# A two-layer encoder trunk with expert layers: plain fp32 products for gathering expert rows and scattering expert outputs

## The chip, the cores and the metric

The kernel runs on one core of a Trainium2 chip. The metric is the device time of one execution in microseconds; for the kernel before, three timed runs are at hand, and one more execution that the hardware profiler took. All rows and stretches shown are of that profiled execution, and their clock starts at its first instruction.

## The reference

A trunk of two layers works on 256 tokens of width 1024, all in float32. Layer 0 mixes by retention and chunked attention, layer 1 by sliding-window attention. Each layer has then a mixture of 16 experts, and after it a gated addition of a side input. What the change touches is the mixture:

```python
g_onehot = jax.nn.one_hot(argmax(g_logits), 4)          # one of 4 groups
top_v, top_i = lax.top_k(e_sel, 2)                      # two of its 4 experts
gates = g_onehot[:, :, None] * (g_w[:, None] * e_gate)[:, None, :]
for gi in range(4):
    hg = jnp.einsum('td,edf->tef', t, w_gate[gi])       # 1024 -> 512
    hu = jnp.einsum('td,edf->tef', t, w_up[gi])
    act = jax.nn.silu(hg) * hu * gates[:, gi, :, None]
    out = out + jnp.einsum('tef,efd->td', act, w_down[gi])   # 512 -> 1024
```

The result of the mixture is added to the residual. Every token goes to two experts, so there are 512 pairs of token and expert.

## The kernel before, in words

**Engines.** The program is written by hand as one instruction list per engine, with semaphores between them; each engine keeps its own order, and nothing is scheduled by a planner. SP issues the weight transfers, TensorE (PE) the products, VectorE (DVE) and ScalarE (ACT) the work between them, GpSimd (POOL) a few powers, ramps and small transfers.

**Weights.** Weights lie in 9 slots of SBUF of 2 MB each (`W`). An expert has three units: gate, up and down. Each is brought in two halves of 1 MB, in an order fixed in the SP list (`load_part`, `load_down`); a half may be written as soon as the products that read its slot before are done (`half_reusable`, semaphores `gate_up_halves`, `gate_up_ready`, `y_halves`, `y_ready`). Transfers therefore run ahead of the products by up to nine units. The down weights of expert 2 lie outside the slots, in `XD` and in the residual `H`, whose content has been copied into the sums by then. All transfers of weights leave through one queue; SP's line 438 is the one that issues a half.

**Routing.** For each of the two token tiles (128 tokens) TensorE makes the logits (L873, L880), VectorE compares and ranks them (`compared`, `ranked`, L1846 and on) and sums of the choices give each pair of token and expert a slot among 512, in order of the experts. VectorE then writes the gather matrix `PH`: token x slot, 1 where the token holds the slot (L1910, L1911). Beside this chain TensorE works on products of the side input (L893).

**Gather.** `gathered_part` (L941) multiplies the normalised rows, 128 tokens x 128 of the columns k, k+8, ..., by `PH` (128 x 512), for k = 0 to 7 and both token tiles, into one bank for each k. The rows are split into two fp32r parts: `HSP[0]` is the high part, the row as ScalarE writes it into an fp32r tile (L1422), and `HSP[1]` the rest, made by VectorE in `rows_low` (L1813), and both are multiplied by the onehots and added in the bank. The eight banks are copied with the norm weights into `XS` (L1447 on ScalarE, L1924 on VectorE). k = 0 to 5 come first; then the first half of expert 0's gate and up products, then k = 6 and 7. `spread` (L969, L971) turns slots and gates of the tokens into rows `SROW` and `WROW`, the same on all partitions.

**Expert loop.** Each expert has a block of 64 slots. ScalarE copies its 64 columns of `XS` to `XE`. `step(e)` on TensorE runs, for expert e: `gate_up` (L981), 16 products of 512 columns with 64 rows of output each, in two column halves of the array; `turned(e)`, the transposes of the hidden rows of expert e - 1 (L990); `scattered(e)`, the scatter of expert e - 2 (L1019); `down` of expert e - 1 (L998), 8 products. The last steps are nested differently: with e = 15 the transposes and the scatter stand between the halves of `gate_up`, and the down products of expert 15 are followed by the scatters of experts 14 and 15.

VectorE works beside it: `slot_gates` makes a gate for each slot (L1969 a match of 512 columns times gates, L1972 its sum); the hidden rows are multiplied by that gate (L1982); `onehots` makes the scatter matrix `PT2`, slot x token (L1976, L1977); `hidden_turned` (L1957) copies the transposed hidden rows. ScalarE makes the tanh (L1477) and copies the outputs of the down products, rounded to fp32r, into `YS` (the copy helper, L1339); VectorE subtracts that from the bank and has the low part (`low_part`, L1987), which lies in `PHT`, the tensor of the gather matrix.

**Scatter.** The output of an expert lies in a bank with its 64 slots twice: partitions 0 to 63 hold columns 0 to 511, the others columns 512 to 1023. `scatter` (L1019) adds it to the token sums, four banks that were opened with zeros (L1008) and seeded with the residual by ScalarE: for each token tile, high and low part, and both halves, a product with 64 rows of contraction. The two halves use different row halves of the array and different banks. That is 8 fp32r products per expert, 16 experts in each of 2 layers. After the last scatter of a token tile (`moe_ready`) its sums are copied to the residual (L1648 on VectorE, the copy helper on ScalarE), transposed (L651) and projected (L666).

Blocks beyond 64 slots of an expert (overflow) have a loop of their own at the end of a layer; in the execution profiled it is not entered.

Of the kernel before, what the change touches and what calls it, by code (L numbers as in the profile page):

```python
# [14 lines left out]
P = 128  # L15
# [139 lines left out]
def odd_group(n):  # L155
# [9 lines left out]
            "vectors": ["spread", "gates", "ag", "act", "first_onehots", "onehots", "hidden", "y_low"]}  # L165
# [31 lines left out]
def build(nc, x, p, norm_mix, norm_ffn, norm_ple, final_norm, even_w_in, even_ret_gn, even_rel_bias, even_w_out,  # L197
# [6 lines left out]
    with ExitStack() as ctx:  # L204
# [27 lines left out]
        with nc.sbuf_tensor("rows_split", [P, 2, TT, D], F32R) as HL:  # L232
            pass
        SROW = sb("token_slots", [P, 2, SEQ])[:, :, :]
        WROW = sb("token_gates", [P, 2, SEQ])[:, :, :]
        YS = sb("expert_outputs", [P, 2, FF], F32R)
# [3 lines left out]
        PTMP = SPREAD[:, 0:SEQ]  # L240
        PT2 = sb("scatter_onehots", [P, 2, SEQ], F32R)
        TH, US = (sb(name, [P, 256])[:, :] for name in ("gate_tanh", "hidden"))
        AG = C[:, C_COSR:C_COSR + 256]
        PHT = sb("gather_onehots", [P, TT, SLOTS], F32R)
# [6 lines left out]
        GATES = sb("slot_gates", [P, 2])  # L251
# [67 lines left out]
        PH = PHT[:, :, :]  # L319
        HSP = [HL[:, part] for part in range(2)]  # L320
# [319 lines left out]
        def _(pe):  # L640
# [224 lines left out]
            def experts(l, u0):  # L865
# [72 lines left out]
                def gathered_part(k, t):  # L938

                    for part in range(2):  # L940
                        mm = pe.matmul(B[rows_bank(k)][:, :], HSP[part][:, t, k:D:KD], PH[:, t, :], start=(t + part == 0),  # L941
                                       stop=(t + part == TT))
                    if t == 1:
                        mm.then_inc(sem("rows_ready"), 1)

                def gathered_first(t):

                    pe.wait_ge(sem("onehots_ready"), 2 * l + t + 1)
                    pe.wait_ge(sem("hs_low"), 3 * l + 1 + t)
                    for k in range(4):  # L950
                        gathered_part(k, t)

                def gathered(k):

                    pe.wait_ge(sem("hs_low"), 3 * l + 3)
# [110 lines left out]
                def step(e):  # L1066
# [16 lines left out]
                    if e >= 1:  # L1083
# [6 lines left out]
                        if v() >= 2 and e < NE:  # L1090
                            pe.wait_ge(sem("ys_low_ready"), v(-1))
# [52 lines left out]
                with pe.If(novf > 0):  # L1144
                    pe.wait_ge(sem("ys_low_ready"), NE * (l + 1))
                    pe.drain().then_inc(ov_sem(l, "used"), 1)
                    with pe.Fori(0, novf) as b:
# [9 lines left out]
                        ov_wait(pe, l, b, "y_low")  # L1157
# [5 lines left out]
                pe.wait_ge(sem("pt2_ready"), NE * (l + 1))  # L1163
                for t in range(TT):
                    scatter(1, t, stop=True, ready=("ys_ready", "ys_low_ready")).then_inc(sem("moe_ready"), 1)
# [156 lines left out]
        def _(act):  # L1322
# [92 lines left out]
            def experts(l, u0):  # L1415
                kn = 3 * l + 1
                for t in range(TT):
# [4 lines left out]
                    act.activation(HSP[0][:, t, :], H[:, t, :], ACT.Copy, scale=rstd(kn, t)).then_inc(sem("hs_high"), 1)  # L1422
# [196 lines left out]
        def _(dve):  # L1619
# [186 lines left out]
            def experts(l, u0):  # L1806
                kn = 3 * l + 1

                def rows_low(t, a=0, b=KD):

                    cols = lambda ap: ap.rearrange("p (m k) -> p m k", k=KD)[:, :, a:b]
                    dve.wait_ge(sem("hs_high"), 2 * l + t + 1)
                    dve.scalar_tensor_tensor(out=cols(HSP[1][:, t, :]), in0=cols(H[:, t, :]), scalar=rstd(kn, t),  # L1813
                                             in1=cols(HSP[0][:, t, :].bitcast(F32)), op0=ALU.mult, op1=ALU.subtract)\
                        .then_inc(sem("hs_low"), 1)

# [72 lines left out]
                rows_low(0)  # L1889
# [8 lines left out]
                rows_low(1, 0, 4)  # L1898
# [20 lines left out]
                rows_low(1, 4, KD)  # L1919
# [47 lines left out]
                def slot_gates(par, col, spread=None, gates=None):  # L1967
# [25 lines left out]
                dve.wait_ge(sem("srow_copied"), l + 1)  # L1993
# [306 lines left out]
```

## Time and profile before

| | us |
|---|---|
| median of 3 timed runs (lowest, highest) | 730.15 (729.17, 730.30) |
| the profiled execution | 729.28 |
| its span, first to last instruction | 727.5 |
| TensorE busy | 707.7 (97%) |
| VectorE busy | 277.8 (38%) |
| ScalarE busy | 149.2 (21%) |
| GpSimd busy | 26.4 (4%) |
| read from HBM | 247.15 MB, 346 GB/s over the span |

The granted TensorE clock is 0.999 of the full 2.4 GHz over the span. The profiled execution is 1.8 us longer than its span, and 0.9 us below the median of the timed runs. Matmuls overlap: the duration of one record includes the time in which the next already runs, so the spacing of starts is what tells the time of a group. A line number can be that of a helper; the names of the tiles then tell what the instruction does.

### The profile page before, as it was taken

The numbers are of one execution on the slowest core, as the hardware profiler recorded it, in microseconds if no ns is written. First come the engines' busy times: TensorE is split into PE (matmuls) and PEld (weight loads), VectorE is DVE, ScalarE is ACT, GpSimd is POOL, SyncE is SP. The second block draws the span as 40 slices with busy tenths as digits, with TensorE's granted clock in tenths as the row PEclk, the third lists the DMA queues.
The fourth block names the chain that finished last, engine by engine and source line by source line (L and its number), as shares of the span: only waits on it lengthen the run. The fifth ranks groups of instructions, "written<-read, shape, count | busy, mean of one in ns | idle before, by whom it ended". The sixth has DMA issues, their size and how long they took to land.

```text
span 727.5 us, 8400 instructions
## 1 busy us (share of the span) xinstructions
PE 707.7 (97%) x3182; PEld 329.6 (45%) x3182; DVE 277.8 (38%) x683; ACT 149.2 (21%) x365; POOL 26.4 (4%) x47
## 2 busy tenths in 40 slices
PE   9999999999999999989999999999999999998996
PEld 6488454564333333333445545464333333332344
DVE  1213361544427242422322557363435424242224
ACT  3000241341111111110331144242111111110132
POOL 0600000000000000000000000000000000000000
PEclk9999999999999999999999999999999999999999
DMA  9997448869999999999999851569999999999941
GB/s 344 373 294 283 183 173 326 341 241 410 425 420 421 419 423 419 421 420 423 401 381 408 341 204 71 185 242 387 421 422 420 421 420 422 421 420 422 405 163 59
DMA packets 50666, 250.89 MB, mean 345 GB/s; under 512 B 4713, under 2 KB 5961, under 8 KB 26049
## 3 DMA queue, kind: packets, MB, share of 16 engines
q1 hardware_dynamic: 48256, 245.04, 84.1%
q0 software_dynamic: 2048, 5.07, 2.3%
q8 instruction: 27, 0.44, 0.2%
q10 hardware_dynamic: 320, 0.22, 0.1%
q14 instruction: 15, 0.11, 0.0%
HBM read 247.15 MB, written 4.73 MB: 346 GB/s over the span
## 4 chain that ended last, share of the span: by engine, by line
PE 85%; DMA 7%; issue 2%; SPq 2%; DVE 2%; ACT 1%; POOLq 0%; POOL 0%; ACTq 0%; DVEq 0%
PE bank L981 26%; PE bank L666 24%; PE bank L998 13%; DMA weights<-in_moe_w_down_dram 7%; PE bank L699 4%; PE bank L1019 4%; PE bank L941 2%; PE bank L893 2%; SPq L438 2%; PE bank L651 2%; PE bank L990 1%; PE bank L679 1%; PE bank L805 1%; PE bank L737 0%; PE bank L1241 0%
## 5 line engine op out<-in xcount | busy, mean ns | idle before, releaser
L981 PE MATMUL bank<-weights,expert_rows 128*64 128x512 f32 x1024 | 227.0, 593 | 6.8 <-DMA weights<-in_moe_w_up_dram 6.8
L666 PE MATMUL bank<-weights,normalised 128*128 128x512 f32 (+1 forms) x448 | 191.4, 580 | 0.9 <-DVE normalised L1637 0.7
L981 PEld LDWEIGHTS bank<-weights,expert_rows 128*64 128x64 f32 x1024 | 74.5, 137 | 149.9 <-issue 149.7
L666 PEld LDWEIGHTS bank<-weights,normalised 128*128 128x128 f32 x448 | 83.1, 190 | 91.4 <-issue 88.5
L998 PE MATMUL bank<-weights,hidden_turned_odd 128*64 128x512 f32 x256 | 58.8, 598 | 0.7 <-DMA weights<-in_moe_w_down_dram 0.7
L998 PE MATMUL bank<-weights,hidden_turned 128*64 128x512 f32 x224 | 51.5, 598 | 1.3 <-DVE hidden_turned L1957 0.6
L1477 ACT ACTIVATE gate_tanh<-bank 128x256 f32<-128x256 f32 x32 | 12.3, 384 | 190.5 <-PE bank L981 190.5
L1339 ACT ACTIVATE expert_outputs<-bank 128x512 fp32r<-128x512 f32 x32 | 19.1, 597 | 123.4 <-PE bank L998 123.4
L1987 DVE TENSOR_TENSOR gather_onehots<-bank,expert_outputs 128x512 fp32r<-128x512 f32 x32 | 22.1, 692 | 55.6 <-ACT expert_outputs L1339 55.5
L1957 DVE COPY hidden_turned<-bank 128x256 f32<-128x256 f32 x16 | 6.8, 424 | 78.5 <-PE bank L990 78.5
L1957 DVE COPY hidden_turned_odd<-bank 128x256 f32<-128x256 f32 x16 | 6.8, 425 | 78.2 <-PE bank L990 78.2
L998 PEld LDWEIGHTS bank<-weights,hidden_turned_odd 128*64 128x64 f32 x256 | 16.9, 136 | 35.0 <-issue 31.8
L1969 DVE SCALAR_TENSOR_TENSOR spread_gates<-token_slots,router_temps,token_gates 128x512 f32<-128x512 f32 x32 | 24.0, 751 | 19.6 <-ACT token_gates L1469 18.6
L998 PEld LDWEIGHTS bank<-weights,hidden_turned 128*64 128x64 f32 x224 | 15.2, 136 | 29.1 <-issue 28.9
L1019 PE MATMUL bank<-expert_outputs,scatter_onehots 64*128 64x512 f32 x128 | 28.4, 441 | 0.0
L699 PE MATMUL bank<-normalised,weights 128*128 128x256 f32 x128 | 28.4, 380 | 0.0
L699 PEld LDWEIGHTS bank<-normalised,weights 128*128 128x128 f32 x128 | 24.1, 190 | 3.7 <-issue 0.5
L1019 PE MATMUL bank<-gather_onehots,scatter_onehots 64*128 64x512 f32 x128 | 25.5, 395 | 0.1
L1339 ACT ACTIVATE expert_rows<-normalised 128x512 f32 (+1 forms) x36 | 20.8, 587 | 11.2 <-issue 7.1
L1972 DVE TENSOR_REDUCE slot_gates<-spread_gates 128x1 f32<-128x512 f32 x32 | 22.0, 686 | 1.1
L990 PEld LDWEIGHTS bank<-constants,hidden 128*128 128x128 f32 x64 | 10.1, 207 | 26.3 <-issue 24.7
L1335 ACT ACTIVATE normalised<-bank,norm_weights 128x128 f32<-128x128 f32 x48 | 13.7, 368 | 33.8 <-PE bank L651 33.5
(265 smaller groups left out, 591.1 us busy)
## 6 DMA issues: line engine op xcount, KB each, us to landing
weights<-in_moe_w_gate_dram SPq DMA_DIRECT2D x64, 1024.0 KB, 16.0
weights<-in_moe_w_up_dram SPq DMA_DIRECT2D x64, 1024.0 KB, 16.9
weights<-in_moe_w_down_dram SPq DMA_DIRECT2D x60, 1024.0 KB, 19.8
weights<-in_even_w_in_dram SPq DMA_DIRECT2D x5, 2048.0 KB, 21.0
weights<-in_ple_w_gate_dram SPq DMA_DIRECT2D x4, 2048.0 KB, 31.3
weights<-in_even_w_out_dram SPq DMA_DIRECT2D x2, 2048.0 KB, 31.3
weights<-in_odd_w_qkv_dram SPq DMA_DIRECT2D x2, 2048.0 KB, 19.6
weights<-in_odd_w_out_dram SPq DMA_DIRECT2D x2, 2048.0 KB, 19.7
```

Of the source, the lines that this page charges most:

```text
L438: sp.dma_start(dst, src).then_inc(done, 16)
L651: mm = pe.transpose(B[banks[half]][:, tok(kk)], H[:, t, 4 * half + kk:D:KD], ident)
L666: mm = pe.matmul(B[bank][:, 0:width], XT[:, k, tok(t)], w[:, k, :], start=(k == 0), stop=(k == KD - 1))
L699: mm = pe.matmul(B[2 * (u % 2) + pair][:, c * SEQ:(c + 1) * SEQ], w[:, k, tok(2 * pair + c)], XT[:, k, :], start=(k == 0), stop=(k == KD - 1))
L981: mm = pe.matmul(bank[j * BLK:(j + 1) * BLK, :].rearrange("p (m f) -> p m f", m=2), rows[:, k, :], W[:, slots, a:a + FF // 2], start=(k == ...
L990: mm = pe.transpose(B[6][:, c * P:(c + 1) * P], US[:, c:2 * P:2], ident)
L998: mm = pe.matmul(bank[half * BLK:(half + 1) * BLK, :], hid[:, 2 * (f % 2) + f // 2, :], rows(f)[:, half * 512:(half + 1) * 512], start=(f ...
L1019: mm = pe.matmul(B[sum_bank(t, half)][:, :], PT2[r, par, tok(t)], (YS, PHT)[part][r, par, :], start=False, stop=stop and part == 1)
L1339: return act.activation(dst, src, ACT.Copy)
L1969: stepped(dve.scalar_tensor_tensor(out=SPREAD, in0=SROW.rearrange("p c s -> p (c s)"), scalar=col, in1=WROW.rearrange("p c s -> p (c s)"), ...
L1972: stepped(dve.tensor_reduce(GATES[:, par:par + 1], SPREAD, AX.X, ALU.add), gates)
L1987: dve.tensor_tensor(PHT[:, par, :], bank[:, :], YS[:, par, :].bitcast(F32), ALU.subtract).then_inc(done, 1)
```

## The change

The rows are no longer split: ScalarE writes the normalised rows once, in float32 (`HN`), `rows_low` is gone, and the gather is one plain float32 product for each k and token tile. The outputs of the down products are copied in float32 and `low_part` is gone. The gate moves from the hidden rows into the scatter matrix: `scatter_gates` matches slots and multiplies by the gates in one instruction of 512 columns, then adds its two halves; `slot_gates` and `onehots` are gone, and the hidden rows are multiplied without a gate. The scatter is one plain float32 product for each token tile and half, with K = 64 as before. In `step(0)` on VectorE the wait for the slot rows (`srow_copied`) comes after the hidden rows instead of before them.

```diff
-        with nc.sbuf_tensor("rows_split", [P, 2, TT, D], F32R) as HL:
+        with nc.sbuf_tensor("normalised_rows", [P, TT, D], F32) as HN:
...
-        YS = sb("expert_outputs", [P, 2, FF], F32R)
+        YS = sb("expert_outputs", [P, 2, FF])[:, :, :]
...
-        PT2 = sb("scatter_onehots", [P, 2, SEQ], F32R)
+        PT2 = sb("scatter_gates", [P, 2, SEQ])[:, :, :]
...
-        PHT = sb("gather_onehots", [P, TT, SLOTS], F32R)
+        PH = sb("gather_onehots", [P, TT, SLOTS])[:, :, :]
...
                 def gathered_part(k, t):
-                    for part in range(2):
-                        mm = pe.matmul(B[rows_bank(k)][:, :], HSP[part][:, t, k:D:KD], PH[:, t, :], start=(t + part == 0),
-                                       stop=(t + part == TT))
+                    mm = pe.matmul(B[rows_bank(k)][:, :], HN[:, t, k:D:KD], PH[:, t, :], start=(t == 0), stop=(t == 1))
...
-                    pe.wait_ge(sem("hs_low"), 3 * l + 1 + t)
+                    pe.wait_ge(sem("rows_normalised"), 2 * l + t + 1)
...
                 def gathered(k):
-                    pe.wait_ge(sem("hs_low"), 3 * l + 3)
...
-                def scatter(par, t, stop=False, ready=None):
-
-                    for part in range(2):
-                        if ready is not None:
-                            pe.wait_ge(sem(ready[part]), NE * (l + 1))
-                        for half in range(2):
-                            r = slice(half * BLK, (half + 1) * BLK)
-                            mm = pe.matmul(B[sum_bank(t, half)][:, :], PT2[r, par, tok(t)], (YS, PHT)[part][r, par, :],
-                                           start=False, stop=stop and part == 1)
+                def scatter(par, t, stop=False):
+
+                    for half in range(2):
+                        r = slice(half * BLK, (half + 1) * BLK)
+                        mm = pe.matmul(B[sum_bank(t, half)][:, :], PT2[r, par, tok(t)], YS[r, par, :], start=False, stop=stop)
                     return mm
...
                 def scattered(e):
-                    pe.wait_ge(sem("ys_low_ready"), NE * l + e - 1)
+                    pe.wait_ge(sem("ys_ready"), NE * l + e - 1)
...
                 pe.wait_ge(sem("pt2_ready"), NE * (l + 1))
+                pe.wait_ge(sem("ys_ready"), NE * (l + 1))
                 for t in range(TT):
-                    scatter(1, t, stop=True, ready=("ys_ready", "ys_low_ready")).then_inc(sem("moe_ready"), 1)
+                    scatter(1, t, stop=True).then_inc(sem("moe_ready"), 1)
...
-                    act.activation(HSP[0][:, t, :], H[:, t, :], ACT.Copy, scale=rstd(kn, t)).then_inc(sem("hs_high"), 1)
+                    act.activation(HN[:, t, :], H[:, t, :], ACT.Copy, scale=rstd(kn, t)).then_inc(sem("rows_normalised"), 1)
...
-                rows_low(0)
...
-                rows_low(1, 0, 4)
...
-                rows_low(1, 4, KD)
...
-                def slot_gates(par, col, spread=None, gates=None):
+                def scatter_gates(par, col, done, matches=None):
                     stepped(dve.scalar_tensor_tensor(out=SPREAD, in0=SROW.rearrange("p c s -> p (c s)"), scalar=col,
                                                      in1=WROW.rearrange("p c s -> p (c s)"), op0=ALU.is_equal, op1=ALU.mult),
-                            spread)
-                    stepped(dve.tensor_reduce(GATES[:, par:par + 1], SPREAD, AX.X, ALU.add), gates)
-
-                def onehots(par, col, done, first=None):
-
-                    stepped(dve.tensor_scalar(PTMP, SROW[:, 0, :], col, None, ALU.is_equal), first)
-                    dve.scalar_tensor_tensor(out=PT2[:, par, :], in0=SROW[:, 1, :], scalar=col, in1=PTMP,
-                                             op0=ALU.is_equal, op1=ALU.add).then_inc(done, 1)
-
-                def hidden_rows(par, gu, done):
-
-                    dve.scalar_tensor_tensor(out=US, in0=AG, scalar=GATES[:, par:par + 1], in1=gu[:, 256:512],
-                                             op0=ALU.mult, op1=ALU.mult).then_inc(done, 1)
-
-                def low_part(bank, par, done):
-
-                    dve.tensor_tensor(PHT[:, par, :], bank[:, :], YS[:, par, :].bitcast(F32), ALU.subtract).then_inc(done, 1)
+                            matches)
+                    dve.tensor_tensor(PT2[:, par, :], SPREAD[:, 0:SEQ], SPREAD[:, SEQ:2 * SEQ], ALU.add).then_inc(done, 1)
+
+                def hidden_rows(gu, done):
+
+                    dve.tensor_tensor(US, AG, gu[:, 256:512], ALU.mult).then_inc(done, 1)
...
-                dve.wait_ge(sem("srow_copied"), l + 1)
-                slot_gates(0, OC[:, 0:1])
...
                 def step(e):
-                    if 2 <= e < NE:
-                        dve.wait_ge(sem("ys_ready"), v - 1)
-                        low_part(B[7], e % 2, sem("ys_low_ready"))
...
-                        hidden_rows(e % 2, gu, sem("act_ready"))
+                        hidden_rows(gu, sem("act_ready"))
+                        if e == 0:
+                            dve.wait_ge(sem("srow_copied"), l + 1)
                         if e >= 2:
                             dve.wait_ge(sem("sc_done"), (NE - 1) * l + e - 1)
-                        onehots(e % 2, OC[:, e:e + 1], sem("pt2_ready"))
-                    if 1 <= e < NE - 1:
-                        dve.wait_ge(sem("pt2_ready"), v + 1)
-                        slot_gates((e + 1) % 2, OC[:, e + 1:e + 2])
+                        if v >= 1:
+                            dve.wait_ge(sem("pt2_ready"), v)
+                        scatter_gates(e % 2, OC[:, e:e + 1], sem("pt2_ready"))
```

## Rows read from the trace of the kernel before

**Rows 1.** The page, chain that ended last: by engine, then by line.

```profile
PE 85%; DMA 7%; issue 2%; SPq 2%; DVE 2%; ACT 1%; POOLq 0%; POOL 0%; ACTq 0%; DVEq 0%
PE bank L981 26%; PE bank L666 24%; PE bank L998 13%; DMA weights<-in_moe_w_down_dram 7%; PE bank L699 4%; PE bank L1019 4%; PE bank L941 2%; PE bank L893 2%; SPq L438 2%; PE bank L651 2%; PE bank L990 1%; PE bank L679 1%; PE bank L805 1%; PE bank L737 0%; PE bank L1241 0%
```

**Rows 2.** Busy time by stretch: stretch, length, PE, PEld, DVE, ACT, POOL, clock, DMA share, GB/s.

```profile
166.70:321.50 154.80, 153.98 (x748) 57.06 (x746) 62.97 (x139) 22.31 (x42) 0.00 (x0) 1.00 1.01 420
321.50:356.70 35.20, 31.24 (x150) 11.70 (x150) 9.43 (x19) 3.97 (x8) 0.09 (x1) 1.00 1.02 414
```

**Rows 3.** Timeline of TensorE over one expert, layer 0: start, length, line, tiles.

```profile
297.27 7.04 PE L981 MATMUL bank<-weights,expert_rows 128*64 128x512 f32 x32
...
304.68 0.50 PE L1019 MATMUL bank<-expert_outputs,scatter_onehots 64*128 64x512 f32 x2
...
305.82 3.65 PE L998 MATMUL bank<-weights,hidden_turned_odd 128*64 128x512 f32 x16
309.31 7.04 PE L981 MATMUL bank<-weights,expert_rows 128*64 128x512 f32 x32
```

**Rows 4.** TensorE's waits (total, times, longest), and its timeline near layer 0's end.

```profile
PE bank L981 <- DMA weights<-in_moe_w_up_dram: 6.8, 6, 1.3
...
PE bank L998 <- DMA weights<-in_moe_w_down_dram: 0.7, 2, 0.3
...
322.22 3.65 PE L981 MATMUL bank<-weights,expert_rows 128*64 128x512 f32 x16 [0.73 <-DMA weights<-in_moe_w_up_dram]
327.18 3.65 PE L981 MATMUL bank<-weights,expert_rows 128*64 128x512 f32 x16 [1.30 <-DMA weights<-in_moe_w_up_dram]
```

**Rows 5.** Groups by line and form: count, busy us, mean ns of a record, idle before.

```profile
L981 PE MATMUL bank<-weights,expert_rows 128*64 128x512 f32 x1024 | 227.0, 593 | 6.8 <-DMA weights<-in_moe_w_up_dram 6.8
...
L941 PE MATMUL bank<-gather_onehots,rows_split 128*128 128x512 f32 x64 | 17.5, 427 | 0.0
```

**Rows 6.** Timeline of TensorE in layer 0's mixer: plain projection, transposes, attention scores.

```profile
83.78 7.13 PE L666 MATMUL bank<-weights,normalised 128*128 128x512 f32 x16
90.75 0.60 PE L747 MATMUL bank<-constants,weights 128*128 128x128 f32 x4
91.28 1.14 PE L737 MATMUL bank<-arena 64*128 64x256 f32 x8
92.34 0.66 PE L747 MATMUL bank<-constants,weights 128*128 128x128 f32 x4
```

**Rows 7.** Timeline of TensorE around layer 0's gather.

```profile
146.18 1.02 PE L893 MATMUL bank<-weights_rest,arena 128*128 128x512 f32 x2
146.64 6.44 PE L941 MATMUL bank<-gather_onehots,rows_split 128*128 128x512 f32 x24
153.01 0.48 PE L1008 MATMUL bank<-zero_column 64*128 64x512 f32 x2
...
157.42 2.34 PE L941 MATMUL bank<-gather_onehots,rows_split 128*128 128x512 f32 x8
159.68 7.09 PE L981 MATMUL bank<-weights,expert_rows 128*64 128x512 f32 x32
```

**Rows 8.** Timeline of the last two scatters of layer 0, TensorE and VectorE.

```profile
353.85 0.49 PE L1019 MATMUL bank<-expert_outputs,scatter_onehots 64*128 64x512 f32 x2
...
355.35 0.50 PE L1019 MATMUL bank<-gather_onehots,scatter_onehots 64*128 64x512 f32 x2
...
355.95 1.29 DVE L1648 COPY residual<-bank 128x512 f32<-128x512 f32 x2 [0.66 <-PE bank L1019]
```

**Rows 9.** Timeline of VectorE and TensorE: routing of layer 0, and the loop's start.

```profile
131.06 1.28 DVE L1813 SCALAR_TENSOR_TENSOR rows_split<-residual,norm_stats,rows_split 128x1024 fp32r<-128x1024 f32 x1 [1.97 <-ACT rows_split L1422]
...
142.00 0.23 DVE L1846 SCALAR_TENSOR_TENSOR router_temps<-bank,norm_stats,router_bias 128x20 f32<-128x20 f32 x1
...
141.63 0.29 PE L880 MATMUL bank<-constants,router_temps 128*128 128x20 f32 x2
...
172.50 0.47 PE L990 MATMUL bank<-constants,hidden 128*128 128x128 f32 x2 [0.16 <-DVE hidden L1982]
```

More of the change, by code:

```diff
@@ L164 @@
             "copies": ["rows", "tanh", "y_out"],
-            "vectors": ["spread", "gates", "ag", "act", "first_onehots", "onehots", "hidden", "y_low"]}
+            "vectors": ["ag", "act", "matches", "onehots", "hidden"]}
 def ov_count(b, step):
@@ L239, in build @@
         SPREAD = sb("spread_gates", [P, 2 * SEQ])[:, :]
-        PTMP = SPREAD[:, 0:SEQ]
-        PT2 = sb("scatter_onehots", [P, 2, SEQ], F32R)
+        PT2 = sb("scatter_gates", [P, 2, SEQ])[:, :, :]
         TH, US = (sb(name, [P, 256])[:, :] for name in ("gate_tanh", "hidden"))
         AG = C[:, C_COSR:C_COSR + 256]
-        PHT = sb("gather_onehots", [P, TT, SLOTS], F32R)
+        PH = sb("gather_onehots", [P, TT, SLOTS])[:, :, :]
         with nc.sbuf_tensor("ple_weights_first", [P, D], F32) as WP0:
@@ L250, in build @@
         WP1 = XD[:, D:2 * D]
-        GATES = sb("slot_gates", [P, 2])
         ZERO = sb("zero_column", [P, 1], F32R)
@@ L318, in build @@
         COMPARED = [ar(4096 + 160 * t, 4256 + 160 * t).rearrange("p (n i j) -> p n i j", n=G + 1, i=E) for t in range(TT)]
-        PH = PHT[:, :, :]
-        HSP = [HL[:, part] for part in range(2)]
         GRID = [SPREAD[:, n * 128:(n + 1) * 128] for n in range(2)]
@@ L1090, in step @@
                         if v() >= 2 and e < NE:
-                            pe.wait_ge(sem("ys_low_ready"), v(-1))
+                            pe.wait_ge(sem("ys_ready"), v(-1))
                         def second():
@@ L1144, in experts @@
                 with pe.If(novf > 0):
-                    pe.wait_ge(sem("ys_low_ready"), NE * (l + 1))
+                    pe.wait_ge(sem("ys_ready"), NE * (l + 1))
                     pe.drain().then_inc(ov_sem(l, "used"), 1)
@@ L1156, in experts @@
                         down(B[7], ACTT[0], lambda f: W[:, 2, f * D:(f + 1) * D], lambda: None, None).then_inc(ov_sem(l, "products"), 1)
-                        ov_wait(pe, l, b, "y_low")
+                        ov_wait(pe, l, b, "y_out")
                         ov_wait(pe, l, b, "onehots")
@@ L1163, in experts @@
                 pe.wait_ge(sem("pt2_ready"), NE * (l + 1))
+                pe.wait_ge(sem("ys_ready"), NE * (l + 1))
                 for t in range(TT):
-                    scatter(1, t, stop=True, ready=("ys_ready", "ys_low_ready")).then_inc(sem("moe_ready"), 1)
+                    scatter(1, t, stop=True).then_inc(sem("moe_ready"), 1)
             def ple(l, gate, halves):
@@ L1807, in experts @@
                 kn = 3 * l + 1
[L1809 to L1815, printed above, removed]
                 def logits_moved(t):
@@ L2005, in step @@
                         hidden_turned((e - 1) % 2, sem("actt_ready"))
-                    if e == 1:
-                        dve.wait_ge(sem("pt2_ready"), v)
-                        slot_gates(1, OC[:, 1:2])
                     if e < NE:
@@ L2014, in step @@
                         dve.wait_ge(sem("ag_ready"), v + 1)
-                        hidden_rows(e % 2, gu, sem("act_ready"))
+                        hidden_rows(gu, sem("act_ready"))
+                        if e == 0:
+                            dve.wait_ge(sem("srow_copied"), l + 1)
                         if e >= 2:
                             dve.wait_ge(sem("sc_done"), (NE - 1) * l + e - 1)
-                        onehots(e % 2, OC[:, e:e + 1], sem("pt2_ready"))
-                    if 1 <= e < NE - 1:
-                        dve.wait_ge(sem("pt2_ready"), v + 1)
-                        slot_gates((e + 1) % 2, OC[:, e + 1:e + 2])
+                        if v >= 1:
+                            dve.wait_ge(sem("pt2_ready"), v)
+                        scatter_gates(e % 2, OC[:, e:e + 1], sem("pt2_ready"))
                 for e in range(6):
                     step(e)
+                dve.wait_ge(sem("pt2_ready"), NE * l + 6)
                 blocks = IOTA16[:, 0:MAXOV].unsqueeze(2).to_broadcast([P, MAXOV, NE])
@@ L2055, in experts @@
                     step(e)
-                for e in (NE - 2, NE - 1):
-                    dve.wait_ge(sem("ys_ready"), NE * l + e + 1)
-                    low_part(B[7 if e < NE - 1 else 4], e % 2, sem("ys_low_ready"))
                 dve.wait_ge(sem("table_ready"), 2 * l + 2)
@@ L2066, in experts @@
                         vector = lambda step: (ov_sem(l, "vectors"), ov_count(b, step)[1])
-                        slot_gates(0, OC2[:, bass.ds(b, 1)], vector("spread"), vector("gates"))
                         ov_wait(dve, l, b, "tanh")
@@ L2071, in experts @@
                         ov_wait(dve, l, b, "ag")
-                        hidden_rows(0, B[4], ov_sem(l, "vectors"))
-                        onehots(0, OC2[:, bass.ds(b, 1)], ov_sem(l, "vectors"), vector("first_onehots"))
+                        hidden_rows(B[4], ov_sem(l, "vectors"))
+                        scatter_gates(0, OC2[:, bass.ds(b, 1)], ov_sem(l, "vectors"), vector("matches"))
                         ov_wait(dve, l, b, "turned")
@@ L2076, in experts @@
                         ov_wait(dve, l, b, "onehots")
-                        ov_wait(dve, l, b, "y_out")
-                        low_part(B[7], 0, ov_sem(l, "vectors"))
                 kn = 3 * l + 2
```

## The prediction

> **What bounds the kernel now.** I read the views from coarse to fine: the page's chain first, then the busy time by stretch, then TensorE's timeline inside one expert, at the end of a layer and at its gather. The chain that ended last is 85% TensorE and 7% DMA, and its DMA share is all one item, the experts' down weights [rows 1]. So the bound is TensorE, with the weight stream close behind it. Where each of them holds is seen in the stretches [rows 2]: from 166.7 to 321.5 us TensorE is busy 153.98 of 154.80 us while the stream runs at 420 GB/s with all DMA engines full; from 321.5 to 356.7 TensorE is busy only 31.24 of 35.20 us. VectorE is busy 62.97 of 154.80 us in the first of them: it has time to spare.
>
> The period of an expert is 12.04 us (start of one gate-and-up group at 297.27 to the next at 309.31) [rows 3]. Its weights are 3 x 1024 x 512 x 4 bytes = 6.29 MB, for which the stream at 420 GB/s needs 15.0 us. TensorE therefore eats into the slots filled ahead, catches up with the stream after about thirteen experts, and only then waits: 6 waits before gate-and-up products and 2 before down products, 6.8 + 0.7 = 7.5 us in both layers together [rows 4]. A wait costs more than its idle time: 322.22 to 327.18 is 4.96 us for a group that takes 3.49 elsewhere (305.82 to 309.31 [rows 3]), so 1.47 us with 1.30 us of idle. With 0.15 us more for each of the 8 the stream costs 8.7 us in all. This is the store that slower TensorE work can draw on, and it is small.
>
> **What one product costs.** A plain fp32 product leaves two matmul records and an fp32r product one: the gate-and-up line issues 2 layers x 16 experts x 16 products = 512 and shows 1024, the gather issues 2 x 8 x 2 x 2 = 64 and shows 64 [rows 5]. A plain record of 512 columns over the whole array takes 0.43 us: 16 of them fill 83.78 to 90.75, 6.97 us with the changeover [rows 6]. So a plain product is 0.86 us. An fp32r product of the gather takes 6.37/24 = 0.265 us in the first batch (146.64 to 153.01) and 2.26/8 = 0.28 in the second (157.42 to 159.68) [rows 7]. Replacing two fp32r products by one plain one therefore replaces about 0.54 us by 0.86. The record durations printed (0.4 and 0.6 us) include the pipeline's tail and are not used.
>
> On the rows, a product of 512 columns costs 0.27 us in one type and 0.86 in the other. The Trainium skill, "TensorE: Matmul & The Clock Gate", section "Step-by-step: what each phase is for", says throughput is purely N cycles, one column of the moving operand per cycle, and makes no exception for the type. By that the sum below would change sign, since the number of products is halved; that is the faster rival.
>
> **The change, part by part.**
>
> *Gather.* Per layer 12 + 4 plain products stand in place of 24 + 8 fp32r ones. First batch: 24 records x 0.43 = 10.3 us against 6.37, +3.9. Second: 8 x 0.43 = 3.4 against 2.26, +1.2. TensorE has nothing to hide this behind: its next products need the gathered rows. I add nothing for the strided weight loads, which the products now cover in less time than 0.43 us. **+5.1 us a layer.** Bounds: 4.9 to 5.5, the upper end if the loads delay each group a little.
>
> *Scatter inside the expert loop.* Before, 8 fp32r products in two row halves of 64: 304.68 to 305.82, 1.14 us for four pairs of records with entry and exit [rows 3]. After, 4 plain products are 8 records, again two halves at a time. The nearest rows are the attention scores, plain fp32 with 64 rows in halves: 8 records of 256 columns in 1.06 us (91.28 to 92.34) [rows 6]; one after another at half of 0.43 us each they would need 1.72, so the halves do run side by side. For 512 columns: 4 pairs x 0.43 = 1.72, plus entry and exit. Lower bound 1.72, upper 1.72 + (1.06 - 0.86) = 1.92; I take 1.87, near the upper end, because the scatter too is entered from transposes and left for products with another tiling. +0.73 per scatter. On this path stand 14 a layer, those of steps 2 to 15: **+10.3 us a layer** (bounds 8.1 to 10.9).
>
> *The last two scatters.* From 353.85 TensorE runs expert 14's scatter and then expert 15's, whose low products wait for VectorE until 355.35; the copy out of the sums begins at 355.95 [rows 8]. The first token tile's sums close with the sixth of eight pairs: 353.85 + 0.1 + 6 x 0.43 + 0.17 of tail = 356.7 instead of about 355.87. **+0.8 us a layer**, the removed wait already in it. The new wait for the high copy stands before expert 15's products; that copy runs under expert 14's scatter, which is now longer (1.8 us).
>
> *Start of the loop.* Hidden rows of expert 0 no longer wait for the spread gates. TensorE idled 0.16 us for them at 172.50 [rows 9]: **-0.15 us.** Behind the moved wait on VectorE stands the copy of turned hidden rows for expert 0; the slot rows it asks for are copied before the tanh that VectorE needs anyway, so it is met. The idle after it, for that copy, stays.
>
> *VectorE's saved work*: the low parts of rows and outputs, the slot gates and one match fall away, an add comes in. I cost it at nothing. In the loop VectorE is idle more than half of the time [rows 2]. Before the gather one might hope for an earlier start, since the low part of half a tile (some 0.7 us, about half of the 1.28 for a whole one) stands ahead of the second comparison. But that comparison begins at 142.00, just after TensorE has the logits, issued at 141.63 [rows 9]; and the last side product (0.43 us from 146.18) holds TensorE until 146.6, when the gather starts anyway [rows 7]. At most 0.1 us is there. Without that cover up to 2 us a layer (1.28 + 0.7) would come back.
>
> *The stream.* The first slots are freed by gate-and-up products that come 3.9 to 5.1 us later, so the stream runs at most 5.1 us later. At the last weights of a layer TensorE is 5.1 + 10.3 = 15.4 us later; the difference, 10.3, exceeds the 4.3 us that it waited per layer. All eight waits vanish, with 6 us of margin: **-8.7 us.** Even at 12.8 us a period TensorE stays quicker than the 15.0 of the stream, so the slots don't starve it. No DMA is added or moved, and SP's and POOL's queues keep their order. What is late next is the down product itself, on TensorE.
>
> **Sum**: 2 x (5.1 + 10.3 + 0.8 - 0.15) - 8.7 = +23.4 us. Against the profiled execution's 729.28 us (span 727.5) this is 752.7; the median of the three runs is 730.15, 0.9 higher, so 753.6.
>
> **Rivals.**
>
> *The stream hides the scatters* (slower, but less). If the end of each layer were set by the stream, only the gather, the tail and the start would count: 2 x 5.75 = +11.5, 741.7 us. For it: 7% of the chain is the down weights, and DMA is full for 190 us. Against: 8.7 us of waits can't cover 32. Chance 0.06.
>
> *The row halves don't overlap in plain fp32* (far slower). Then a scatter is 8 x 0.43 + 0.15 = 3.6 us, +1.73 for each of 32: +55, 809 us. Against: the scores' 1.06 us. Chance 0.04.
>
> *A plain product costs no more than one fp32r product* (faster). The place is the gather and the scatter on TensorE; the price is one record spacing instead of two. The gather then falls by half, -4.3 us a layer, of which 3.2 comes before the first slot is freed; the scatters fall by 0.48 each (half of 1.14 less entry and exit), but those 6.7 us end as longer waits, since the stream moves only by 3.2; the tail gives 0.5. 2 x -3.7 = -7.4, 722.7 us. It decides from the point where two plain records of 512 columns take less than two fp32r products (0.53 us). This is the skill's rule of N cycles at work in this kernel. Against: the two records at 0.43 us, at 512 products of the same width. Chance 0.04.
>
> *VectorE's relief was on the path*: up to 2 us a layer at the gather and nothing else gained, 753.6 - 4 = 749.6. It lies within the range; chance 0.04.
>
> The forecast itself has 0.82. Its own bounds: scatters 2 x (8.1 to 10.9) gives -4.4 to +1.2, gathers -0.4 to +0.8, and some of the 8.7 us could stay (up to +2): 748.5 to 757.5. The range goes a little further on both sides for runs that differ and for the middle of the neighbouring cases: 746 to 759; outside it lie 741.7, 809 and 722.7, with 0.14. About 0.2% is what a measurement of this kernel can tell from no change, 1.5 us; only the faster rival and a sliver of unnamed cases lie on that side or within it: faster 0.04, same 0.01, slower 0.95.
>
> **What would show it.** The gather line should have 64 records, as now, but 24 of them from start to next group in 10.3 us. The scatter line should have 256 records, as now, and 1.87 us from its first record to the first down record (1.14 now); the expert period should be 12.8 us. The waits of TensorE for up and down weights should be gone, and the DMA rate in the loop should stay near 420 at first and sag towards the end. VectorE's busy time should fall by some 60 us without an effect. The forecast is wrong if the period stays at 12.0, if it rises above 14, or if waits for weights above 2 us remain.

## The result and the profile after

The kernel after takes 754.74 us (median of 4 runs, 754.12 to 755.06) against 729.66 for the kernel before in the same comparison (728.91 to 730.30): a ratio of 1.0343, 95% interval 1.0325 to 1.0361, or +25.1 us. The forecast was 753.6 us, within 746 to 759.

The page of the kernel after: span, busy times, and the chain that ended last by engine and by line.

```profile
span 752.3 us, 8287 instructions
...
PE 741.4 (99%) x3182; PEld 332.4 (44%) x3182; DVE 215.8 (29%) x581; ACT 149.3 (20%) x365; POOL 26.4 (4%) x47
...
PE 95%; issue 2%; DVE 1%; DMA 1%; ACT 1%; SPq 0%; POOLq 0%; POOL 0%; DVEq 0%; ACTq 0%
PE bank L974 29%; PE bank L662 24%; PE bank L991 15%; PE bank L1009 8%; PE bank L936 4%; PE bank L695 4%; PE bank L889 2%; PE bank L983 2%; PE bank L647 1%; DMA weights<-in_even_w_in_dram 1%; PE bank L675 1%; PE bank L733 0%; PE bank L1231 0%; PE bank L757 0%; PE bank L743 0%
```

These answer to [rows 1]. The down weights (7% of the chain before) are gone from the chain, the scatter (L1009) has gone from 4% to 8% and the gather (L936) from 2% to 4%. TensorE's record count is the same, 3182: gather and scatter have half as many products as before, each with two records instead of one. VectorE lost 62 us of work and the kernel is slower.

The groups by line, with their counts, answer to [rows 5]; the full list of TensorE's waits, longest first, to [rows 4].

```profile
L974 PE MATMUL bank<-weights,expert_rows 128*64 128x512 f32 x1024 | 226.3, 593 | 0.0
...
L1009 PE MATMUL bank<-expert_outputs,scatter_gates 64*128 64x512 f32 x256 | 63.1, 613 | 0.0
...
L936 PE MATMUL bank<-gather_onehots,normalised_rows 128*128 128x512 f32 x64 | 28.6, 599 | 0.0
```

```profile
PE bank L801 <- DVE weights L1641: 1.0, 1, 1.0
PE bank L1243 <- ACT arena L1329: 0.7, 1, 0.7
PE bank L662 <- DVE normalised L1627: 0.7, 2, 0.3
PE bank L991 <- DVE hidden_turned L1936: 0.6, 1, 0.6
PE bank L991 <- issue: 0.6, 1, 0.6
PE bank L869 <- ACT normalised L1325: 0.4, 1, 0.4
PE bank L662 <- ACT arena L1329: 0.2, 1, 0.2
PE bank L1231 <- DVE normalised L2140: 0.2, 1, 0.2
```

The gate-and-up products no longer idle at all (0.0 against 6.8 us), and no transfer stands among the waits. TensorE's timeline of layer 0: around the gather and at the loop's start, over one expert, and at the end.

```profile
145.63 1.02 PE L889 MATMUL bank<-weights_rest,arena 128*128 128x512 f32 x2
146.49 10.46 PE L936 MATMUL bank<-gather_onehots,normalised_rows 128*128 128x512 f32 x24
156.88 0.48 PE L1001 MATMUL bank<-zero_column 64*128 64x512 f32 x2
...
161.29 3.83 PE L936 MATMUL bank<-gather_onehots,normalised_rows 128*128 128x512 f32 x8
165.05 7.09 PE L974 MATMUL bank<-weights,expert_rows 128*64 128x512 f32 x32
...
323.06 7.04 PE L974 MATMUL bank<-weights,expert_rows 128*64 128x512 f32 x32
...
330.46 1.99 PE L1009 MATMUL bank<-expert_outputs,scatter_gates 64*128 64x512 f32 x8
332.38 3.65 PE L991 MATMUL bank<-weights,hidden_turned 128*64 128x512 f32 x16
335.87 7.04 PE L974 MATMUL bank<-weights,expert_rows 128*64 128x512 f32 x32
...
365.59 3.70 PE L1009 MATMUL bank<-expert_outputs,scatter_gates 64*128 64x512 f32 x16
369.31 1.16 PE L647 MATMUL bank<-constants,residual 128*128 128x128 f32 x8
```

Against [rows 7] the first batch of the gather grows from the last side product on: 146.18 to 153.01 was 6.83 us, 145.63 to 156.88 is 11.25, +4.4. The second batch: 157.42 to 159.68 was 2.26, 161.29 to 165.05 is 3.76, +1.5. Against [rows 3] a scatter takes 1.92 us instead of 1.14, and the expert period 12.81 instead of 12.04, +0.77. Against [rows 8] the last two scatters with what follows to the transposes take 3.72 us; before it was 353.85 to 356.70, 2.85: +0.87. One difference means nothing: the kernel after is 0.55 us ahead of the kernel before when the gather begins. It gains that in the first 15 us, where both have the same instructions and wait for the first input rows; among the kernels run here that point moves by 0.9 us.

### The profile page after: what moved, and what is told of

Read it like the earlier page. It is cut to its first block, busy times and chain, and to the rows that moved or that the text cites. A ratio compares the mean times of both kernels' runs of the same rounds, so it can differ in the third digit from the quotient of the medians.

```text
span 752.3 us, 8287 instructions
## 1 busy us (share of the span) xinstructions
PE 741.4 (99%) x3182; PEld 332.4 (44%) x3182; DVE 215.8 (29%) x581; ACT 149.3 (20%) x365; POOL 26.4 (4%) x47
## 4 chain that ended last, share of the span: by engine, by line
PE 95%; issue 2%; DVE 1%; DMA 1%; ACT 1%; SPq 0%; POOLq 0%; POOL 0%; DVEq 0%; ACTq 0%
PE bank L974 29%; PE bank L662 24%; PE bank L991 15%; PE bank L1009 8%; PE bank L936 4%; PE bank L695 4%; PE bank L889 2%; PE bank L983 2%; PE bank L647 1%; DMA weights<-in_even_w_in_dram 1%; PE bank L675 1%; PE bank L733 0%; PE bank L1231 0%; PE bank L757 0%; PE bank L743 0%
## 5 line engine op out<-in xcount | busy, mean ns | idle before, releaser
L1009 PE MATMUL bank<-expert_outputs,scatter_gates 64*128 64x512 f32 x256 | 63.1, 613 | 0.0
L1329 ACT ACTIVATE expert_outputs<-bank 128x512 f32<-128x512 f32 x32 | 19.1, 597 | 142.3 <-PE bank L991 142.3
L1009 PEld LDWEIGHTS bank<-expert_outputs,scatter_gates 64*128 64x128 f32 x256 | 22.2, 186 | 21.0 <-issue 17.6
L936 PE MATMUL bank<-gather_onehots,normalised_rows 128*128 128x512 f32 x64 | 28.6, 599 | 0.0
L936 PEld LDWEIGHTS bank<-gather_onehots,normalised_rows 128*128 128x128 f32 x64 | 19.9, 314 | 7.6 <-DVE gather_onehots L1891 0.5
L1971 DVE SCALAR_TENSOR_TENSOR constants<-gate_tanh,bank 128x256 f32<-128x256 f32 x32 | 13.2, 412 | 30.1 <-ACT gate_tanh L1467 30.1
```

Source lines behind the costliest of these rows:

```text
L936: mm = pe.matmul(B[rows_bank(k)][:, :], HN[:, t, k:D:KD], PH[:, t, :], start=(t == 0), stop=(t == 1))
L1329: return act.activation(dst, src, ACT.Copy)
L1971: dve.scalar_tensor_tensor(out=AG, in0=TH, scalar=1.0, in1=gu[:, 0:256], op0=ALU.add, op1=ALU.mult)\
```

## Experiments

All of them were compared with the kernel before on the chip they ran on. Its median there was 729.46 us for the gather alone, the scatter alone, the gates on the hidden rows and the order of the halves; 728.78 for the two extra products, single fp32r and the contiguous weights; and 729.50 for one row half and the earlier first rows.

**Gather alone.** The rows are written once in float32 and gathered by plain products; gates, low parts and scatter are as before.

```diff
-                    for part in range(2):
-                        mm = pe.matmul(B[rows_bank(k)][:, :], HSP[part][:, t, k:D:KD], PH[:, t, :], ...)
+                    mm = pe.matmul(B[rows_bank(k)][:, :], HN[:, t, k:D:KD], PH[:, t, :], start=(t == 0), stop=(t == 1))
```

> The gather alone in plain fp32, scatter and gates as before. By my theory (TensorE's path, and a stream that follows the first freed slots) the gather costs 4.4 us in its first batch and 1.5 in its second per layer. The stream starts to refill 4.4 us later, so part or all of the 1.5 falls into the waits for weights that are still there: 2 x (4.4 to 5.9) = +9 to +12 us, 739 to 742, and the waits of TensorE for weights fall from 7.5 us to about 4.5 but do not vanish. If the gather's cost were hidden by the stream: 730.

Measured: 739.33 us, ratio 1.0140 (1.0123 to 1.0157), +9.9 us. The gather takes 10.4 and 3.76 us, as in the full change. Its waits for weights:

```profile
PE bank L978 <- DMA weights<-in_moe_w_up_dram: 5.4, 5, 1.3
```

They fell from 6.8 us to 5.4 and did not vanish. So the gather's 5.9 us a layer show nearly in full (4.9), because the stream moves with them: in layer 0 the wait for the last down weights ends at 357.74 us instead of 351.99.

**Scatter alone.** Gates in the scatter matrix and one plain product for each token tile and half; rows split and gathered as before.

> The scatter alone in plain fp32 with the gates in its matrix, gather split as before. By my theory 14 scatters of +0.78 us, +0.9 at the layer's end, -0.2 at its start and 4.4 us of waits used up, twice: +14 us, 744, with no wait for weights left. If the stream hid the scatters: 731. If the whole cost of 11 us a layer were to show: 753. The sum of this run's and the gather run's cost should be the 25 us of the full change or a little below.

Measured: 743.18 us, ratio 1.0192 (1.0175 to 1.0209), +13.7 us, and no wait for weights is left. The scatter takes 1.92 us (312.12 to 314.04):

```profile
312.12 1.99 PE L1013 MATMUL bank<-expert_outputs,scatter_gates 64*128 64x512 f32 x8
314.04 1.51 PE L995 MATMUL bank<-weights,hidden_turned_odd 128*64 128x512 f32 x6
```

The two costs add up to 23.6 us, 1.5 less than the full change. Both kernels draw on the same store of waits, the first a little of it, the second all; the full change can use it only once.

**How large the store is.** An unread plain product is added to the kernel before ahead of each expert's transposes, 15 times a layer, with 128 and with 512 columns.

```diff
+                    if e >= 2:
+                        for _ in range(1):
+                            pe.matmul(B[6][:, 0:128], ident, XS[:, 0, 0:128], start=True, stop=True)
                     turned_back().then_inc(sem("act_turned"), 1)
```

The other run has 0:512 in place of both 0:128.

> The kernel before with one more plain product of 128 columns, its result never read, ahead of the transposes of each expert from the second on, 15 a layer. It should take 0.2 to 0.3 us, 3 to 4.5 us a layer, about what TensorE waits for weights in each layer (4.4). By my theory it is hidden: +0 to +1 us, 730, and the waits for weights shrink to near nothing. If the waits are no store that can be drawn on: +6 to +9.

> The same with 512 columns, 0.86 us, 12.9 us a layer. By my theory 4.4 of them are hidden: 2 x 8.5 = +17 us, 747. If nothing is hidden +26, 756; if the stream hid it all, 730.

TensorE's timeline with 128 columns (one transposes group with the extra product ahead of it), then with 512.

```profile
305.89 0.49 PE L1057 MATMUL bank<-normalised,constants 128*128 128x128 f32 x2
306.21 0.40 PE L990 MATMUL bank<-constants,hidden 128*128 128x128 f32 x2
306.54 0.50 PE L1019 MATMUL bank<-expert_outputs,scatter_onehots 64*128 64x512 f32 x2
```

```profile
312.91 1.13 PE L1057 MATMUL bank<-normalised,constants 128*128 128x512 f32 x2
313.88 0.39 PE L990 MATMUL bank<-constants,hidden 128*128 128x128 f32 x2
314.19 0.50 PE L1019 MATMUL bank<-expert_outputs,scatter_onehots 64*128 64x512 f32 x2
```

The transposes alone lead to the scatter in 0.43 us. With 128 columns it is 0.65: +0.22, 6.6 us for 30 of them. Measured: 729.09 us, ratio 1.0001 (0.9992 to 1.0010). Nothing of 6.6 us is seen, and the waits for up weights fall from 6.8 to 1.8 us. With 512 columns it is 1.28: +0.85, 25.5 us for 30. Measured: 745.42 us, ratio 1.0222 (1.0208 to 1.0237), +16.6 us. No wait for the experts' weights is left. So 25.5 - 16.6 = 8.9 us are absorbed (8.2 to 10.3 by the interval of the ratio) and the rest shows. That is the kink the forecast rests on, measured with work that has nothing to do with the change.

**VectorE's relief.** The kernel after, with VectorE's former work for the gates: a gate per slot, the hidden rows multiplied by it, plain onehots in float32 for the scatter.

> The kernel after, but with the gates on the hidden rows and plain onehots in the scatter matrix, all of VectorE's work for that as before. By my theory VectorE's relief is worth nothing but the 0.2 us at the start of each expert loop: 755.1, the same within 0.2%, with VectorE busy some 35 us more. If the relief was on the path (up to 2 us a layer): 757 to 759.

Measured: 754.82 us, ratio to the kernel before 1.0350 (1.0333 to 1.0367); the kernel after has 1.0343 (1.0325 to 1.0361).

```profile
PE 741.9 (99%) x3182; PEld 333.2 (44%) x3182; DVE 252.9 (34%) x645; ACT 149.4 (20%) x365; POOL 26.5 (4%) x47
```

VectorE is busy 252.9 us instead of 215.8, and the time is the same. Where the gates are multiplied in does not matter for the time. The run gives back 37 of the 62 us; the low parts of the rows and of the outputs stay away, and no run gives those back. What their removal was worth ahead of the gather is read from the traces: in the kernel before, TensorE waits there for VectorE's routing once, 0.22 us in layer 1.

```profile
468.65 0.40 PE L880 MATMUL bank<-constants,router_temps 128*128 128x20 f32 x2 [0.22 <-DVE router_temps L1820]
```

In the kernel after this wait is gone.

**Do the row halves run side by side?** First the order of the four products was changed: both token tiles of one half, then both of the other.

```diff
-                    scatter(e % 2, 0)
-                    scatter(e % 2, 1).then_inc(sem("sc_done"), 1)
+                    for half in range(2):
+                        r = slice(half * BLK, (half + 1) * BLK)
+                        for t in range(TT):
+                            mm = pe.matmul(B[sum_bank(t, half)][:, :], PT2[r, e % 2, tok(t)], YS[r, e % 2, :], ...)
```

> The kernel after, with the four products of each scatter in the loop ordered by row half instead of by token tile. If the two row halves run side by side only when neighbours in the list use different halves, only the middle two products overlap now: 2.6 us instead of 1.7 plus the same entry, +0.86 for each of 30 scatters, +26 us, 780 us, and an expert period of 13.7 us. If TensorE pairs them whatever the order, or if they never overlapped: 755.

Measured: 754.64 us, ratio 1.0345 (1.0328 to 1.0363). The group is as long as ever:

```profile
318.54 1.99 PE L1055 MATMUL bank<-expert_outputs,scatter_gates 64*128 64x512 f32 x8
320.46 3.65 PE L991 MATMUL bank<-weights,hidden_turned_odd 128*64 128x512 f32 x16
```

The first case of the expectation, 780 us with pairs only between neighbours in the list, is ruled out. The run does not tell whether the halves overlap whatever the order, or never do. So all products of the scatter, and the zeros that open the sums, were put on one half; the sums are then other ones, but the work has the same size. The edit to the scatter:

```diff
-                        r = slice(half * BLK, (half + 1) * BLK)
+                        r = slice(0, BLK)
```

> The kernel after, with all products of the scatter, and the zeros that open the sums, on the upper row half of the array: both column halves of the sums then get the same half of the outputs, so the sums are other ones; work and instructions are the same in number and size. The order of the products did not matter, which leaves two readings. If each row half has a sequence of its own and the two run side by side, all 8 records now queue in one: 8 x 0.43 + 0.2 = 3.6 us instead of 1.92, +1.7 for each of 32 scatters, +54 us, 809 us. If a record with 64 rows simply takes half of the time, in whichever half: 755, unchanged.

Measured: 809.92 us, ratio 1.1104 (1.1087 to 1.1121).

```profile
306.83 3.70 PE L1009 MATMUL bank<-expert_outputs,scatter_gates 64*128 64x512 f32 x8
310.46 3.65 PE L991 MATMUL bank<-weights,hidden_turned_odd 128*64 128x512 f32 x16
```

The same 8 records take 3.63 us instead of 1.92, +1.71, and 32 x 1.71 = 54.7 explains the +55.2 us on the kernel after. Each row half works through records of its own, in parallel with the other, and neither of the two orders tried costs more than the other. This was the far slower rival (809 us), and it is now shown what keeps it away.

**The faster rival's price.** The four tiles of the kernel after in fp32r: one product where there were two parts, no low parts.

> The kernel after with its four tiles of gather and scatter in fp32r: one product per k and token tile and no low parts, so half of the fp32r products of before. This is the price of the faster rival. TensorE's period falls to about 11.5 us, but the stream can only move with the first freed slot, 3 us earlier: 2 x -3.5 = -7 us, 722.7, with waits for weights of some 20 us. If TensorE's work alone set the time, 4 + 7 us a layer would be gained: 708.

Measured: 726.20 us, ratio 0.9963 (0.9948 to 0.9977), -2.6 us, against the 7 us of gain expected. First TensorE's waits, then its timeline at the gather.

```profile
PE bank L974 <- DMA weights<-in_moe_w_up_dram: 22.4, 18, 2.1
PE bank L1001 <- ACT normalised L1437: 1.7, 2, 0.9
...
PE bank L991 <- DMA weights<-in_moe_w_down_dram: 1.0, 2, 0.5
```

```profile
146.02 3.47 PE L936 MATMUL bank<-gather_onehots,normalised_rows 128*128 128x512 f32 x12
150.42 0.48 PE L1001 MATMUL bank<-zero_column 64*128 64x512 f32 x2 [0.93 <-ACT normalised L1437]
150.96 3.65 PE L974 MATMUL bank<-weights,expert_rows 128*64 128x512 f32 x16
```

Most of the saved time turned into waits for weights, as expected: 23.4 us of them against 7.5 before. But a quicker gather also ran into the copies of its banks on ScalarE (0.93 us), and the stream moved less than the gather: the last down weights landed at 351.49 us instead of 351.99.

**Freeing slots earlier.** The kernel before, with the gather of k = 5 behind the first half of expert 0.

```diff
-                for k in range(4, 6):
-                    gathered(k)
+                gathered(4)
...
                 first_rows(0)
+                gathered(5)
                 open_sums(1)
```

> The kernel before, with the gather of k = 5 moved behind the first half of expert 0's gate and up products, so that these start some 0.9 us earlier and the first slots are freed earlier. If the stream's end follows the first freed slots in this direction too: -0.9 us a layer, 728. If something else holds the stream at that point (the run with single products freed them 2.5 us earlier and its last down weights landed only 0.5 us earlier): -0.3 us at most in each layer, or none: 729 to 730.

Measured: 730.30 us, ratio 1.0008 (0.9999 to 1.0017): no gain. SP's issues in this kernel, then in the kernel before.

```profile
155.95 0.33 SPq L438 DMA_DIRECT2D weights<-in_moe_w_up_dram  x1
...
158.80 0.33 SPq L456 DMA_DIRECT2D residual<-in_moe_w_down_dram  x1
163.50 0.33 SPq L438 DMA_DIRECT2D weights<-in_moe_w_up_dram  x1
```

```profile
157.12 0.33 SPq L438 DMA_DIRECT2D weights<-in_moe_w_up_dram  x1
...
158.67 0.33 SPq L456 DMA_DIRECT2D residual<-in_moe_w_down_dram  x1
163.38 0.33 SPq L438 DMA_DIRECT2D weights<-in_moe_w_up_dram  x1
```

The first slots are refilled 1.2 us earlier, but the next two issues are where they were, at the seeded sums (158.8) and at expert 1's first half (163.5). The stream is held by a row of such releases, and moving one of them alone gives nothing. A later gather moves them all: in the kernel after, the same three issues stand at 160.99, 162.55 and 168.74, 3.9 to 5.4 us later.

**Contiguous weights for the gather.** The kernel before, with the split rows stored by k, so that TensorE reads them without a stride.

```diff
-                        mm = pe.matmul(B[rows_bank(k)][:, :], HSP[part][:, t, k:D:KD], PH[:, t, :], ...)
+                        mm = pe.matmul(B[rows_bank(k)][:, :], HSP[part][:, t, k * P:(k + 1) * P], PH[:, t, :], ...)
...
-                    act.activation(HSP[0][:, t, :], H[:, t, :], ACT.Copy, ...)
+                    act.activation(HSP[0][:, t, :].rearrange("p (k m) -> p k m", k=KD), H[:, t, :].rearrange("p (m k) -> p k m", k=KD), ACT.Copy, ...)
```

> The kernel before, with the split rows stored so that the 128 columns of one k lie side by side: the gather's weights are then read without a stride, ScalarE and VectorE read the residual with one. In the kernel before a strided load takes 329 ns against 184 for one without a stride, and the fp32r records start 0.24 us apart where 512 columns at half of 0.43 us would be 0.21. If the load sets that spacing, the gather falls by 0.8 us in its first batch and 0.3 in its second, and the stream moves with it: -2 us, 727.7. If it does not: 729.7, same. If the strided reads slow ScalarE and VectorE ahead of the gather: up to +1.

Measured: 732.33 us, ratio 1.0051 (1.0036 to 1.0065), +3.6 us: slower, and by more than the +1 that was allowed for. TensorE's timeline at the gather and in layer 1's routing, then VectorE's low part of a tile.

```profile
144.98 0.40 PE L930 MATMUL bank<-router_temps,constants 128*128 128x16 f32 x2 [0.97 <-DVE router_temps L1865]
...
147.71 6.05 PE L941 MATMUL bank<-gather_onehots,rows_split 128*128 128x512 f32 x24
153.69 0.48 PE L1008 MATMUL bank<-zero_column 64*128 64x512 f32 x2
...
471.11 0.40 PE L880 MATMUL bank<-constants,router_temps 128*128 128x20 f32 x2 [1.99 <-DVE router_temps L1821]
```

```profile
131.91 2.10 DVE L1814 SCALAR_TENSOR_TENSOR rows_split<-residual,norm_stats,rows_split 128x1024 fp32r<-128x1024 f32 x1 [2.98 <-ACT rows_split L1422]
```

The first batch falls by 0.4 us only (5.98 against 6.37, both by the printed starts), so the stride of the load was a small part of its spacing. VectorE's low part, which now steps through the residual, takes 2.10 us instead of the 1.28 of [rows 9], and ScalarE's high part, which does so too, 2.17 instead of 1.16; TensorE waits for the routing behind them, 1 us in layer 0 and 3 in layer 1. The run does not separate the two. It bears on the forecast too: the cover under which I had put VectorE's low parts in the kernel before is real but thin. In layer 0 the second comparison begins 1.76 us after the issue of the logits (141.46 to 143.22) instead of 0.37 (141.63 to 142.00); TensorE idles 0.97 us of the 1.39 added, so some 0.4 us were covered. In layer 1 TensorE waited 0.22 us in the kernel before already.

No kernel run here beats the kernel before with all of its computation.

## Why the prediction was right

- **Two records at 0.43 us for a plain product**: right. The counts stay at 256 and 64, and with one part in fp32r the first batch of the gather takes 3.1 us (from 146.42, when the side records are over, to 149.49), with the same 12 products in plain float32 10.4. The rule of N cycles, which makes no exception for the type (the Trainium skill, "TensorE: Matmul & The Clock Gate", "Step-by-step: what each phase is for"), does not hold here for float32: by it the change would have come out faster. The measured product took 0.87 us (10.4/12) where the fp32r one took 0.26 (3.1/12).
- **Gather, +5.1 us a layer**: too small; it is 5.9, beyond my upper bound of 5.5 as well. In the first batch I took the printed start of its first record, 146.64, as the end of what went before. But two side records from 146.18 last until 147.04; the fp32r batch took 5.97 us, not 6.37. In the second I took 2.26/8 as a spacing. About 0.3 us of it is entry and exit of the group, which stay: in the kernel after, 3.76 us are 8 x 0.43 and 0.32 more, and its first two records start 0.66 us apart.
- **Scatter, +0.73, bounds 0.58 to 0.78**: the upper bound, +0.78 (1.92 us). 14 a layer by the period make 10.8 instead of 10.3 (and 14 x 0.73 is 10.2). That the halves overlap was right, and is shown by the run on one half.
- **The last two scatters, +0.8; the start, -0.15**: +0.87 and, from 174.04 to the transposes at 177.63, 3.59 us against 3.82 before, -0.23.
- **VectorE's relief, nothing**: right to some tenths. Giving back the work on the gates changed nothing; the low parts were not given back, and the wait that their removal can have ended is 0.22 us.
- **The store, -8.7**: right in kind; 8.9 by the run with 512 columns. Hence 2 x (5.9 + 10.8 + 0.87 - 0.23) - 8.9 = +25.8, against 25.1 measured (plus or minus 1.3) and 23.4 forecast. Gather and scatter were both sized too small, so the errors add up, to 2.4 us; the range had room for them. (The bounds of the single terms add up to 748.8 to 757.6, not to 748.5 to 757.5.)
- **The price of the faster rival, 722.7**: too low. Without the second part it measured 726.2: the stream came 0.5 us earlier in layer 0, not 3.2. That later slots delay the stream nearly in full, and earlier ones hardly help it, was not in the prediction: the gather alone put the last down weights off by 5.75 of its 5.9 us. The forecast needed only the first of the two.
- **The rival in which the stream hides the scatters, 741.7**: what it can hide is 8.9 of 34.7 us. The stream now has time to spare. SP's issues of the last down weights of layer 0 in the kernel after:

```profile
321.56 10.46 SPq L434 DMA_DIRECT2D weights<-in_moe_w_down_dram  x4
```

The last is issued by 332.0 us and its half is first used at 363.8, 31.8 us later; in the kernel before the same two points were 327.3 and 351.99, 24.7 us apart, and there TensorE waited for the landing. If the transfer takes as long in both, about 7 us are to spare (an estimate from these four times; the forecast had 6).

## What to carry to other kernels

Before merging a high and a low fp32r product into a plain float32 one, compare the spacing of starts: here it was two records at 0.43 us for two at 0.23 to 0.25. Half the products and 62 us less on another engine said nothing about the time, since the limiting engine was left with more work. A second limit close behind the first absorbs added work once and up to a size that an unread product of known length measures well; here most of the work saved there was lost to waits too. And a group's time has an entry in it: divide only what comes after.

## What the runs showed of the hardware

- Two row halves of the array of 64 rows each take their products in sequences of their own. 8 records of 512 columns in plain fp32 take 1.92 us on two halves, in both orders of issue that were tried, and 3.63 us on one.
- Weight loads with a stride of 8 elements take 313 to 331 ns, without one 184 to 190. In fp32r their removal moved the spacing of the gather by only some 0.02 us a record, although a load is longer than the spacing.
- A VectorE instruction that reads 1024 elements of the residual in steps of 8 takes 2.10 us, and 1.28 in order; a ScalarE copy of the same elements 2.17 and 1.16.
